# Queries and keys of the second block: channel weights in ScalarE's copy, inverse root multiplied on GpSimd

## The reference, cut to what matters

```python
def _rms(x, g):                       # over the 64 channels of one head
    y = x * lax.rsqrt(jnp.mean(x * x, axis=-1, keepdims=True) + EPS)
    return y * g

fq = _rms(heads(fq, FOX_HEADS, HEAD_DIM), fox_qk_g[l, 0])
fk = _rms(heads(fk, FOX_HEADS, HEAD_DIM), fox_qk_g[l, 1])
dq = _rms(dq, diff_qk_g[l, 0])        # and dk with diff_qk_g[l, 1]
s = jnp.einsum('bhqd,bhkd->bhqk', qi, k) / sqrt(64)   # then softmax, then times v
```

## Time and profile before

| what | us |
|---|---|
| median of three runs (924.36 to 926.34) | 924.53 |
| span of the profiled execution, first to last instruction | 920.9 |
| median less span: what lies around the span | 3.6 |
| TensorE matmul busy | 890.8 (97% of the span) |
| VectorE busy | 679.2 (74%) |
| ScalarE busy | 542.1 (59%) |
| GpSimd busy | 290.6 (32%) |
| mean granted TensorE clock | 0.996 |

### The profile page before, as it was taken

The page is one execution under the profiler, slowest core; times in us unless marked ns, Lnnn a source line. Parts: engine busy times, 40 slices in busy tenths (PEclk is TensorE's granted clock), DMA queues, the critical chain, the costliest instruction groups (busy, mean ns, idle before and its releaser), DMA issues.

```text
span 920.9 us, 17831 instructions
## 1 busy us (share of the span) xinstructions
PE 890.8 (97%) x7390; PEld 858.8 (93%) x7390; DVE 679.2 (74%) x870; ACT 542.1 (59%) x840; POOL 290.6 (32%) x266
## 2 busy tenths in 40 slices
PE   5999999999999999999999999988999999999998
PEld 5899999999999999999999999977888989999998
DVE  5988997888686868768888767678995587755442
ACT  4467666556877864477556444567687674544431
POOL 5600003543467821176754111120003552112100
PEclk9999999999999999999999999999999999999999
DMA  8754556666676778854888887423233449755560
GB/s 364 293 215 167 192 174 242 230 229 229 230 300 226 258 275 304 288 199 142 308 309 283 304 318 286 162 92 138 93 137 122 154 151 332 273 205 174 175 226 23
DMA packets 36112, 203.02 MB, mean 220 GB/s; under 512 B 4928, under 2 KB 6080, under 8 KB 17216
## 3 DMA queue, kind: packets, MB, share of 16 engines
q1 hardware_dynamic: 36032, 201.89, 60.9%
HBM read 200.82 MB, written 1.05 MB: 219 GB/s over the span
## 4 chain that ended last, share of the span: by engine, by line
PE 65%; issue 13%; DVE 12%; ACT 5%; POOL 4%; DMA 1%; SPq 0%; POOLq 0%; ACTq 0%; DVEq 0%
PE acc L1145 58%; ACT w_hi L721 2%; DVE ada_w L1463 2%; DVE w_lo L1405 2%; DVE cv L1608 2%; POOL rt L618 1%; POOL ul L624 1%; DMA ada_w<-in_ada_tiles 1%; PE m L1228 1%; DVE qk L1709 1%; DVE fr L1429 1%; POOL maps L665 1%; PE acc L1110 1%; DVE maps L1703 1%; DVE rt L1704 1%
## 5 line engine op out<-in xcount | busy, mean ns | idle before, releaser
L1405 DVE TENSOR_TENSOR w_lo<-raw,w_hi 128x2048 fp32r<-128x2048 f32 x141 | 324.5, 2302 | 130.1 <-ACT w_hi L721 130.1
L1145 PE MATMUL acc<-uh,w_hi 128*128 128x256 f32 x1320 | 374.3, 284 | 4.2 <-POOL ul L624 2.1
L1145 PE MATMUL acc<-ul,w_hi 128*128 128x256 f32 x1320 | 367.4, 278 | 0.0
L1145 PE MATMUL acc<-uh,w_lo 128*128 128x256 f32 x1320 | 367.4, 278 | 0.0
L721 ACT ACTIVATE w_hi<-raw 128x2048 fp32r<-128x2048 f32 x141 | 266.3, 1888 | 77.4 <-PE acc L1145 77.4
L1145 PEld LDWEIGHTS acc<-uh,w_hi 128*128 128x128 f32 x1320 | 250.0, 189 | 10.8 <-issue 5.4
L1145 PEld LDWEIGHTS acc<-ul,w_hi 128*128 128x128 f32 x1320 | 249.6, 189 | 0.4 <-issue 0.2
L1145 PEld LDWEIGHTS acc<-uh,w_lo 128*128 128x128 f32 x1320 | 249.6, 189 | 0.0
L1145 PE MATMUL acc<-hidh,w_hi 128*128 128x256 f32 x432 | 119.2, 276 | 0.0
L1145 PE MATMUL acc<-hidl,w_hi 128*128 128x256 f32 x432 | 119.2, 276 | 0.0
L1145 PE MATMUL acc<-hidh,w_lo 128*128 128x256 f32 x432 | 119.2, 276 | 0.0
(11 more groups left out here) (368 smaller groups left out, 1579.1 us busy)
## 6 DMA issues: line engine op xcount, KB each, us to landing
raw<-in_tiles SPq DMA_DIRECT2D x137, 1024.0 KB, 5.5
colw<-in_ada_cols SPq DMA_DIRECT2D x80, 512.0 KB, 5.3
ada_w<-in_ada_tiles SPq DMA_DIRECT2D x8, 1024.0 KB, 17.2
raw<-in_rest SPq DMA_DIRECT2D x4, 768.0 KB, 5.2
cact<-in_c_rows SPq DMA_DIRECT2D x2, 512.0 KB, 4.3
xT<-in_x SPq DMA_DIRECT2D x1, 1024.0 KB, 7.4
first_w<-in_tiles SPq DMA_DIRECT2D x1, 1024.0 KB, 17.2
out<-xT SPq DMA_DIRECT2D x8, 128.0 KB, 3.7
```

What stands on the lines that cost most here:

```text
L1145: ins = pe.matmul(o, l, r, start=(s.k == 0 and i == 0 and not j), stop=(s.last and i == s.kts - 1 and j == 2))
L1405: dve.tensor_tensor(lo, raw_of(n), hi.bitcast(F32), ALU.subtract).then_inc(S("lo_ready"), 1)
```

## The change

ScalarE's second pass over a query or key bank now multiplies by the channel weights while it copies. The eight pairs of multiplications by the inverse root leave VectorE, and GpSimd does them with a plain two-operand product. VectorE's last refinement raises a new semaphore `qr_done`, on which GpSimd waits, and is no longer linked. GpSimd's part stands ahead of its other work of the same half step. Ahead of its copy into `fcum_t` GpSimd now waits for its own products, and after it for the copy.

```diff
+        QK_BASE = {"dq": 0, "dk": 4, "fq": 8, "fk": 12}
+        QK_GAIN = {"dq": small[:, 7:8], "dk": qk_gain[:, 3:4], "fq": small[:, 6:7], "fk": qk_gain[:, 1:2]}
...
# GpSimd, in the loop over steps and halves
+                    prev = steps[n - 1] if n else None
+                    if nb == 1 and prev and prev.kind in QK_BASE:
+                        jq += 1
+                        pool.wait_ge(S("qr_done"), jq)
+                        for half in range(NB):
+                            b = QK_BASE[prev.kind] + NB * prev.j + half
+                            pool.tensor_tensor(qk[:, b, :], qk[:, b, :], rt[:, half, :], ALU.mult).then_inc(S("qk_done"), 1)
...
                     pool.wait_ge(S("nlf_done"), 1)
+                    pool.wait_ge(S("qk_done"), NB * jq)
...
+                    pool.wait_ge(S("fcum_zero"), 1)
...
# ScalarE
-                        act.activation(qk[:, b, :], ps, ACT.Copy).then_inc(free, 1)
+                        act.activation(qk[:, b, :], ps, ACT.Identity, scale=QK_GAIN[s.kind]).then_inc(free, 1)
...
# VectorE
-                        link(dve.scalar_tensor_tensor(qr, qt, 1.5, qr, ALU.add, ALU.mult))
-                        base, gcol = {"dq": (0, small[:, 7:8]), "dk": (4, qk_gain[:, 3:4]), "fq": (8, small[:, 6:7]),
-                                      "fk": (12, qk_gain[:, 1:2])}[prev.kind]
-                        for half in range(NB):
-                            b = base + NB * prev.j + half
-                            dve.scalar_tensor_tensor(qk[:, b, :], qk[:, b, :], gcol, rt[:, half, :], ALU.mult, ALU.mult)\
-                               .then_inc(S("qk_done"), 1)
+                        dve.scalar_tensor_tensor(qr, qt, 1.5, qr, ALU.add, ALU.mult).then_inc(S("qr_done"), 1)
```

More of the change, by code:

```diff
@@ L653, in _ @@
             lo_part(U1 + KB - 1)
+            jq = 0
             for n in range(NS):
@@ L948, in _ @@
                     if s.kind in ("dq", "dk", "fq", "fk"):
-                        b = {"dq": 0, "dk": 4, "fq": 8, "fk": 12}[s.kind] + NB * s.j + nb
+                        b = QK_BASE[s.kind] + NB * s.j + nb
                         if nb == 0 and QK_ORDER.index((s.kind, s.j)):
```

## The result

The changed kernel takes 932.06 us (median of 4 runs, 931.41 to 935.29), against 924.44 us for the kernel before (4 runs, 921.92 to 926.34). The ratio is 1.0096, with a 95% interval of 1.0076 to 1.0116: some 7.6 us slower. The prediction was 930.8 us, slower, within 926.5 to 934.5.

A forecast was written before the change was run, and what follows sets the result against it. TensorE, 97% busy, was taken as the bound, with VectorE's latency costing at three points. Terms 3.2 - 0.75 + 0 + 2.25 + 1.65 = +6.3 us, clock 0, on the median 924.53 gave 930.8 us; range 926.5 to 934.5.

The forecast's parts named there:

- The exclusion: GpSimd's products and VectorE's split, each reading two SBUF tensors, run one after the other; pairs end about 3.5-3.6 us after L1704.
- The sign of splits of 2.5 to 2.7 us: In slots 7 to 19, VectorE's splits would take 2.5 to 2.7 us instead of 2.29.
- Slot 6: TensorE starts the maps of slot 6 at 625.6 instead of 622.41, after slot 5's late products: +3.2 us.
- The detour over ScalarE's shared tile: Slot 3: ScalarE's next root waits for GpSimd's pair, delaying that root and slot 5's L1704 by 0.6 us.
- Gates: `dta` comes 2.45 us late rather than 3.2; TensorE's wait there shrinks from 1.8 to 1.05 us: -0.75.
- Slot 12: TensorE came 3.1 us after the pair's end, at 649.38; the later pair is still in time: 0.
- Slots 16 and 20: Late pairs delay TensorE's start by +2.25 us at slot 16 and +1.65 us more at slot 20.
- The clock: TensorE's clock, 643 to 649 us: one fall before and after, so 0, bounds ±1.7 us; dearer rival 932.5 to 935 us, 23%.
- VectorE's load: Whole stage: load costs nothing by itself elsewhere; rival that it was the bound: 2.9 us gain, 921.7 us, 7%.
- The relief: 7.0 us of products leave VectorE; TensorE can gain at most 2.9 us: 0.3 slot 20, 0.87 `dta`, 1.7 clock.

The follow-up runs named there:

- the dummies: Changed kernel plus 12 products of constants, whose result nothing reads, on TensorE ahead of slot 6, where it waits: 929.88 us, ratio 1.0075.
- the three groups: Timing groups of the follow-up kernels, each on another chip in 5 rounds, beside the kernel before: 923.18, 924.55 and 924.63 us for the latter.
- second root tile in the changed kernel: Changed kernel with the second pair's root put in `cct`, so ScalarE need not wait for the first pair's products: 929.84 us, ratio 1.0059.
- three query pairs: Against the kernel before, GpSimd multiplies only the query pairs of slots 7, 13 and 17; VectorE keeps the others: 921.72 us, ratio 0.9971.

## Why the prediction was right, and where it was not

- **The exclusion**, on which all rested, holds, and holding the split back (slot 5, then everywhere) shows it: 1.40 us for a pair in place of 3.38 with nothing else changed. The pair ends 3.5 us behind the last refinement in slot 5 (622.73 to 626.19) and 3.6 in slot 15 (668.84 to 672.46), as worked out. The sign of splits of 2.5 to 2.7 us did not come: they took 2.28, because a small operation (L1538, in slot 11 L1725) stood ahead of them and waited in their place, and in slots 17 and 19 the split went first; the end of the pair is the same either way. The Trainium skill ("SBUF — State Buffer", section "Who interferes with whom") says that whichever issues first holds the shared port pair for its whole instruction, and lists `tensor_scalar` among VectorE's operations that can contend for it. The trace agrees, down to L1538, a `tensor_scalar` that waits (0.67 us for 0.23) though its operands are tiny.
- **Slot 6**: 3.1 us measured, 3.2 forecast. The detour over ScalarE's shared tile made the last refinement 0.5 us later against the sums of slot 4, where 0.6 was forecast.
- **Gates**: the wait for `dta` went from 1.8 to 1.1 us, as forecast (1.05).
- **Slot 12**: 0 forecast. Right only while the clock falls ahead of it; where it doesn't, TensorE waits 1.3 us. The step took TensorE's arrival at 649.38 as given, when it was itself 1.7 us late for a fall.
- **Slots 16 and 20**: 2.3 and 1.9 us, forecast 2.25 and 1.65.
- **The clock** is the term that was mis-sized: "one such fall after the change as before it, so 0". The two profiles of the changed kernel have three and four. The fall at slot 6 alone costs 2.6 us, by the dummies; the later ones some 1.3 us each by the table. The other executions, at 0.993 to 0.994, had fewer than the profiled one, and the median came out 1.3 us over the forecast. How many each had is not listed, but the mean granted clock gives an estimate. A line through the times of the 62 executions of the kernel before in the three groups, and one through the nine of the changed kernel, each against the time lost to the clock (one less the mean granted clock, times the span), give 922.1 and 928.5 us at full clock, and 0.7 us for each us lost. By this estimate, good to about 1 us, some 6.4 us of the loss are on the path, where the sum without its clock term had 6.3, and some 2.4 us are the clock's, where it had 0. That the path's figure is met so closely is partly luck: the sum lacks the wait of 1.3 us at slot 12, and it took slot 20 from a trace in which a fall hid 0.6 us of VectorE's lateness. The Trainium skill's warning of long gaps ("TensorE: Matmul & The Clock Gate", section "Why this matters for your kernels") was the better guide here than my cancelling of two falls: both profiles of the changed kernel have one at the gap of slot 6, and the one with dummies there has none. But falls came after gaps of 2 us too, and in other executions not.
- **VectorE's load**, which "costs nothing by itself elsewhere", was judged wrongly, and no term of the sum showed it, because in the changed kernel the late pairs set the time at slots 16 and 20. The relief showed as soon as GpSimd got only pairs that could be late: 2.8 us under before, where the prediction had at most 2.9 us for it, 1.7 of them for the clock.

## What to carry to other kernels

Before work moves to GpSimd, ask what VectorE runs in the same microseconds: where both read two SBUF tensors they took turns here, and a product of 0.74 us ended behind VectorE's longest operation. Give GpSimd results that have a slot to spare and keep the ones that the next engine stands waiting for; the same move that lost 1% with all eight pairs won 0.3% with three. When a wait on TensorE grows, count the fall of the clock behind it as a cost of its own, and remember that a fall in the old trace hides waits that will show once it goes.

## What was not expected of the hardware

- A fall of TensorE's clock ahead of a wait can cost nothing: in three of the profiles (split held back in slot 5, second root tile in the changed kernel, three query pairs) it fell between 616 and 620 us, and the maps of slot 6 still started when their data came. The same kernel then shows a wait shorter by what the fall took. Waits are to be read with the start of what they delay, not alone.
- A VectorE operation on 128x2 values (L1538) took 0.67 us beside a GpSimd product and 0.23 us alone; it waited for the first product, and so the split behind it did too. In slot 11 a VectorE operation with one operand out of a bank (L1724) took 0.42 us while a product ran, as it did before, and a copy from SBUF to SBUF behind it (L1725) 0.29 us instead of 0.22.
- Two VectorE products of 128x256 without a per-partition factor take 0.76 us, two with it 0.88, and one of 128x512 with it 0.75.
- The kernel before, in 31 executions on one chip, ran from 921.44 to 928.23 us, at mean granted clocks from 1.00 to 0.992. A fall like that of the earlier trace rows costs up to 1.7 us, so the spread is that of some four falls, which some executions have and others do not.
